# Hybrid HGRN2 and pooling block on one core: a third pair of banks for the transposes of the first tokens

## What is computed

```python
z = jnp.concatenate([meta, x], axis=1)
h = rms_norm(z, norm_w[l])
p = (h @ w_in[l] + b_in[l]).astype(f32)
q, fz, iv, g_hg, u, g_pool, m_hg, m_pool = jnp.split(p, split_at, axis=-1)
...
y_hg = (o * jax.nn.silu(g_hg)) @ w_down_hg[l].astype(f32)
...
merged = jax.nn.sigmoid(m_hg) * y_hg + jax.nn.sigmoid(m_pool) * y_pool
z = z + (merged @ w_out[l].astype(f32)).astype(z.dtype)
return rms_norm(z, final_norm_w)[:, N_META:]
```

## Time and profile before

| what | value |
|---|---|
| median of 3 runs | 1047.99 us (1047.74 to 1049.66) |
| the profiled execution's own time | 1047.79 us |
| its span, first to last instruction | 1046.1 us |
| granted clock of PE, mean | 0.999 |
| PE busy | 1025.0 us (98%) |
| DVE busy | 779.7 us (75%) |
| ACT busy | 491.4 us (47%) |
| POOL busy | 98.1 us (9%) |

### The profile page before, as it was taken

One profiled execution on the slowest core, in us unless ns is written; L12 is line 12 of the kernel. 1 busy time (PEld: TensorE's weight loads), 2 busy tenths in 40 slices (PEclk: granted clock), 3 DMA queues, 4 the chain that ended last, 5 costly groups with the idle time before them and its releaser, 6 DMA issues.

```text
span 1046.1 us, 18490 instructions
## 1 busy us (share of the span) xinstructions
PE 1025.0 (98%) x7252; PEld 835.8 (80%) x7252; DVE 779.7 (75%) x1276; ACT 491.4 (47%) x834; POOL 98.1 (9%) x166
## 2 busy tenths in 40 slices
PE   7999999999999999999999999999999999999997
PEld 7767888888888888878888887788887887787886
DVE  7989787878686868786676877764569789978234
ACT  7764636363636363544353433434457346345222
POOL 6200000000010101020101010011100110000111
PEclk9999999999999999999999999999999999999999
DMA  7221111111020202121312122228322684555233
GB/s 276 51 81 63 42 61 42 62 39 64 29 75 21 81 22 82 41 82 52 101 41 91 60 91 81 71 99 294 116 96 101 207 316 158 177 189 181 71 101 131
DMA packets 36630, 105.65 MB, mean 101 GB/s; under 512 B 4640, under 2 KB 4640, under 8 KB 36544
## 3 DMA queue, kind: packets, MB, share of 16 engines
q1 hardware_dynamic: 22352, 66.14, 19.5%
q0 software_dynamic: 8528, 27.31, 7.2%
q10 hardware_dynamic: 5664, 11.02, 2.9%
HBM read 79.28 MB, written 25.17 MB: 100 GB/s over the span
## 4 chain that ended last, share of the span: by engine, by line
PE 81%; DVE 13%; issue 3%; ACT 2%; DMA 1%; POOL 0%; DVEq 0%; SPq 0%; ACTq 0%
PE acc L1372 61%; PE acc L1259 8%; PE levels L1425 2%; DVE w_lo L1687 1%; PE miscs L1447 1%; PE miscs L1458 1%; PE miscs L1459 1%; DVE r_lo L2240 1%; PE acc L1317 1%; PE miscs L1259 1%; PE levels L1259 1%; DVE att L1841 1%; DVE qx L1860 1%; PE miscs L1465 1%; PE miscs L1438 1%
## 5 line engine op out<-in xcount | busy, mean ns | idle before, releaser
L1372 PE MATMUL acc<-r_hi,w_hi 128*128 128x512 f32 x1112 | 308.0, 399 | 4.1 <-ACT second L837 1.7
L1372 PE MATMUL acc<-r_lo,w_hi 128*128 128x512 f32 x1112 | 304.9, 393 | 0.5 <-DVE r_lo L2240 0.4
L1372 PE MATMUL acc<-r_hi,w_lo 128*128 128x512 f32 x1112 | 298.5, 390 | 0.5 <-DVE w_lo L1687 0.5
L1372 PEld LDWEIGHTS acc<-r_lo,w_hi 128*128 128x128 f32 x1112 | 206.5, 188 | 50.1 <-issue 4.9
L1372 PEld LDWEIGHTS acc<-r_hi,w_lo 128*128 128x128 f32 x1112 | 208.6, 188 | 45.6 <-DVE w_lo L1687 1.0
L1372 PEld LDWEIGHTS acc<-r_hi,w_hi 128*128 128x128 f32 x1112 | 201.6, 188 | 48.7 <-ACT second L837 3.1
L752 ACT ACTIVATE w_hi<-sum 128x512 fp32r<-128x512 f32 x156 | 97.8, 628 | 164.1 <-DVE sum L1721 85.7
L1687 DVE TENSOR_TENSOR w_lo<-sum,w_hi 128x512 fp32r<-128x512 f32 x156 | 106.3, 685 | 58.7 <-ACT w_hi L752 58.3
L1687 DVE TENSOR_TENSOR w_lo<-raws,w_hi 128x512 fp32r<-128x512 f32 x120 | 82.1, 686 | 54.8 <-ACT w_hi L752 54.6
L752 ACT ACTIVATE w_hi<-raws 128x512 fp32r<-128x512 f32 x120 | 74.5, 623 | 26.1 <-PE acc L1372 24.4
L837 ACT ACTIVATE second<-acc,bias 128x512 f32<-128x512 f32 x31 | 21.2, 684 | 57.8 <-PE acc L1372 57.7
(11 more groups left out here) (301 smaller groups left out, 1364.6 us busy)
## 6 DMA issues: line engine op xcount, KB each, us to landing
raws<-in_wstream SPq DMA_DIRECT2D x88, 512.0 KB, 3.6
xin<-in_x SPq DMA_DIRECT2D x8, 512.0 KB, 6.1
a_spill<-gt POOLq DMA_DIRECT2D x16, 256.0 KB, 3.5
c_spill<-pg POOLq DMA_DIRECT2D x16, 256.0 KB, 2.7
stage<-a_spill ACTq DMA_DIRECT2D x4, 1024.0 KB, 13.9
smh_spill<-zq POOLq DMA_DIRECT2D x16, 256.0 KB, 2.4
gate_in<-smh_spill SPq DMA_DIRECT2D x16, 256.0 KB, 5.2
part_spill<-zq POOLq DMA_DIRECT2D x16, 256.0 KB, 5.7
```

The lines of the kernel that those rows point to most:

```text
L1372: ins = pe.matmul(bank[:, :], weights, moving, start=n == 0 and i in (0, 1, 5 if p < EARLY else 3), stop=n == 3 * KH - 1, skip_group_check ...
```

## The change

Three engines get another order in the head; no arithmetic is added or taken away apart from two warm-up matmuls.
- Tile 3 is turned into `acc[3]` and `acc[2]`, two banks of the products. Tile 4 goes into the banks of tile 1 (`lev`, `small`), and from there on the even and odd tiles have changed places: 5 and 7 in `misc`, 6 and 8 in `lev` and `small`. `h_transposes(3)` no longer waits for another tile, and tile 4 waits, as tile 3 did, for tile 1. Product (0, 1) now also waits for `h_lo` of tile 3, since it overwrites `acc[2]`.
- DVE scales the rows of tile 3 before it splits tile 1, and the rows of tile 4 before it splits tile 2; the copies `b11_copy(3)` and `b11_copy(4)` come after other splits; `x_mean(5)` moves behind `low(1)`.
- ACT squares tile 5 after `high(1)` in place of before the copies of tile 3.
- PE issues four warm-up matmuls before product (0, 0) in place of six.

```diff
+        def tile_banks(i):
+
+            return (acc[3], acc[2]) if i == 3 else h_banks[i % 2 if i < 3 else (i + 1) % 2]
...
             first_tile(2)
-            square_x(5)
             first_tile(3)
             high(0)
             first_tile(4)
             high(1)
+            square_x(5)
             square_x(6)
...
                 elif p == 0 and i == 1:
                     pe.wait_ge(S["h_copied"], 4)
+                    pe.wait_ge(S["h_lo"], 3)
...
                     pe.wait_ge(S["hm_copied"], 1)
-                elif i > 2:
-                    pe.wait_ge(S["h_copied"], i - 2)
-                    pe.wait_ge(S["h_lo"], min(i - 2, 4))
+                elif i > 3:
+                    had = (1, 2, 4, 5, 6)[i - 4]
+                    pe.wait_ge(S["h_copied"], had)
+                    pe.wait_ge(S["h_lo"], min(had, 4))
...
-            keep_warm(6)
+            keep_warm(4)
             product(0, 0)
...
+            h_row(3)
             b11_low(1)
             b11_copy(1)
+            x_mean(4)
             b21_low(1)
-            h_row(3)
-            x_mean(4)
+            h_row(4)
             b11_low(2)
             b11_copy(2)
+            b11_low(3)
             b21_low(2)
-            h_row(4)
-            x_mean(5)
-            b11_low(3)
             low(0)
-            b11_copy(3)
             b11_low(4)
             b21_low(3)
+            b11_copy(3)
             b11_copy(4)
             b21_low(4)
             low(1)
+            x_mean(5)
             x_mean(6)
             h_row(5)
```

More of the change, by code:

```diff
@@ L761, in banks_of @@
             def banks_of(i, rows):
-                return [b[:, :].rearrange("p (k t) -> p k t", k=KH)[:, :, 0:rows] for b in h_banks[i % 2]]
+                return [b[:, :].rearrange("p (k t) -> p k t", k=KH)[:, :, 0:rows] for b in tile_banks(i)]
             def meta_tile():
@@ L1385, in h_transposes @@
                     pe.wait_ge(S["hm_copied"], 1)
-                elif i > 2:
-                    pe.wait_ge(S["h_copied"], i - 2)
-                    pe.wait_ge(S["h_lo"], min(i - 2, 4))
+                elif i > 3:
+                    had = (1, 2, 4, 5, 6)[i - 4]
+                    pe.wait_ge(S["h_copied"], had)
+                    pe.wait_ge(S["h_lo"], min(had, 4))
                 for k in range(NK):
                     o = (k % 4) * P
-                    ins = pe.transpose(h_banks[i % 2][k // 4][:, o:o + rows], hrow[0:rows, i % 2, k * P:(k + 1) * P],
+                    ins = pe.transpose(tile_banks(i)[k // 4][:, o:o + rows], hrow[0:rows, i % 2, k * P:(k + 1) * P],
                                        ident[0:rows, 0:rows])
@@ L1606, in banks_of @@
             def banks_of(i):
-                return [b[:, :].rearrange("p (k t) -> p k t", k=KH) for b in h_banks[i % 2]]
+                return [b[:, :].rearrange("p (k t) -> p k t", k=KH) for b in tile_banks(i)]
             def b11_low(i):
```

## The result

The changed kernel took 1050.19 us, median of 21 runs (1048.49 to 1051.37); the kernel before, run beside it, took 1048.78 us (1047.70 to 1049.66, 21 runs). The ratio is 1.0014, with a 95% interval from 1.0007 to 1.0020: slower by 1.4 us, inside 0.2%. The profiled execution took 1051.11 us, with a span of 1049.4 us: 3.3 us more than the span of before.

A forecast was written before the change was run, and what follows sets the result against it. The prediction took the head to be bounded by DVE before PE takes over; 0.63 us on PE's side and 0.65 to 0.8 on DVE's, side by side, gave +0.7 on 1047.99, so 1048.7 us, range 1046.9 to 1050.6.

The forecast's parts named there:

- The early start: Head: DVE scales tile 4 at 16.42 in place of 18.01, so product (0, 0) starts 1.97 us earlier, at about 19.55.
- What DVE still owes: Before tile 5: DVE's remaining work makes PE wait 0.8 us for `low(1)`, leaving about 1.0 of the 1.97 us.
- The mean that was moved: `x_mean(5)` on DVE: its power on POOL comes into the open, `h_row(5)` 0.89 us later, PE 0.63 us behind.
- POOL's queue: Three masks behind tile 5's late power hold up tile 6's: `h_row(6)` 1.4 us late, PE loses nothing more or 0.1.
- The wait for ACT at tile 8's split: DVE's old 0.62 us wait at 36.45 for ACT's last copy of tile 8, forecast to be filled by DVE's delay.
- The sum: Whole kernel: +0.7 us, from 0.63 on PE's side and 0.65 to 0.8 on DVE's, running side by side.
- The rival of the clock: PE's waits between 23.5 and 26.4 us make its clock fall: +2.55 us in all, 1050.5; chance 0.05.
- The prediction's own sign of the clock: Transposes after PE's stall before tile 5 longer than 1.1 us would show that the clock had fallen.
- hidden: Rival: POOL's power is done before DVE reaches `h_row(5)`, so nothing visible changes: -0.1 us, 1047.9; chance 0.08.
- slow: Rival: tile 5's power on POOL takes 1.52 us, 0.97 more on tile 5: +1.65 us, 1049.6; chance 0.07.
- the early start did not pass: Rival: PE's earlier start in the head passes through in full, -1.97 us, 1046.0; chance 0.05.
- the first mask held nothing: Rival: POOL's first mask holds `h_row(5)` until 25.27, 0.22 us more on tile 5: +0.9 us, 1048.9; chance 0.05.

The follow-up runs named there:

- E9: The changed kernel with thirteen warm-up matmuls in place of four ahead of product (0, 0): 1050.48 us, ratio 1.0016 to the kernel before.
- E1: The changed kernel with `x_mean(5)` moved up on DVE, ahead of `b21_low(4)`: 1048.98 us, ratio 1.0005 to the kernel before.
- E2: The changed kernel with POOL's three masks ahead of `x_rstd(5)` in place of behind it: 1049.95 us, ratio 1.0010 to the kernel before.
- E8: The changed kernel measured once more, with nothing altered: 1049.36 us, ratio 1.0009 to the kernel before.
- E5: The changed kernel with six throw-away warm-up matmuls ahead of tile 5's transposes: 1048.96 us, ratio 1.0008 to the kernel before.
- E10: The changed kernel with six throw-away matmuls ahead of tile 5's transposes, as E5, for more runs: 1049.53 us, ratio 1.0007 to the kernel before.
- E3: The changed kernel with twelve throw-away warm-up matmuls ahead of tile 5's transposes: 1051.55 us, ratio 1.0029 to the kernel before.
- E7: The changed kernel with `x_mean(5)`, `low(1)` and the masks earlier, `b11_copy(3)` and `b21_low(4)` later: 1047.67 us, ratio 0.9990 to the kernel before.

## Why the prediction was right, and where its size was off

**The verdict.** Within 0.2%, as forecast with 0.90. The measured step is +1.4 us, twice the forecast of +0.7, and the median of 1050.19 lies inside the range, near its end.

**The early start.** Right. Product (0, 0) at 19.64 (19.55 said), `h_row(4)` at 16.42 (16.42 said). Its worth was put at nothing, since PE's holes were DVE's work in another order; E9's head shows that.

**What DVE still owes.** Right. The two small means began at 24.21, where `x_mean(5)` was put at 24.23. PE waited 0.57 us for `low(1)` (0.8 said).

**The mean that was moved.** Right, and it is the whole of the regular loss. `h_row(5)` at 25.02 (25.05 said), tile 5 turned at 26.36 (26.39 said), the power 0.55 as taken from the idle row and not 1.52; PE stood 1.28 us (1.57 said). E1 undoes this step alone, and the head returns to that of before (+0.05).

**POOL's queue.** Right in the places: `h_row(6)` at 27.21 (27.3 said) behind a wait of 0.84, masks of 0.30 and 1.47 ahead of it. Its cost beside PE's delay is at most a tenth (E2). The wait for ACT at tile 8's split is gone in E8, as said; in the profile of the change it stands at 38.68 (0.88 us), where the slowed PE had made ACT's copy later still.
The Trainium skill (SBUF — State Buffer, "Who interferes with whom") would have had the first mask, begun at 24.95, hold `h_row(5)` for its whole length. The trace disagrees for that mask: the scaling began at 25.02 and took 1.28, and the second mask, begun at 25.20 under the scaling, was the one held; the third only queued behind it.

**The sum.** Right where the clock holds: +0.62 to +0.79 in the heads of E2, E5, E8, E9 and E10. As a forecast of the median it is short, at least in part because it took the fall of the clock as a rival for all runs or none, with 0.05, when it comes in a part of the executions: without the five runs of low clock the change has a median of 1049.59, 0.81 above before, and with them 1.41.

**The rival of the clock.** This is the step that was mis-sized. Its argument against itself, that holes of 1.77 and 1.06 us had left the transposes at 1.09, read those holes ahead of warm-ups; the new ones lie just behind the first products. Whether that difference is what decides, no run tests. The prediction's own sign of the clock, transposes of over 1.1 us behind the stall, came in the profile of the change (1.19 for tile 5, 1.39 for tile 6) and not in E8 (1.09 for tile 5). Runs with a mean clock of 0.997 or less number 11 of 43 in the three sets whose profile stands 1.28 us before tile 5 (the change, E8, E2), and none of 166 in all the others, before included. In the change these five have a median of 1050.59 and the sixteen others 1049.59; in E8, 1050.46 and 1049.08. So the counted runs are 1.0 to 1.4 us longer than the rest, which is no clean price, since the rest holds uncounted falls, that of the profiled run at least. In the head of the profiled one the fall cost 1.5 (2.20 - 0.7), against the 1.85 taken from the earlier trace rows, where the granted clock reads 1.00 and no row showed the lower level.
That the hole before tile 5 is what lets the clock fall is well supported, as E1, E3, E5, E9 and E10 each shorten or fill it and have no such run (none of 51); but only one trace shows where a fall lies. How much of the median's excess over +0.7 the clock makes is not settled: the very same kernel stood 1.41 us above before in its first comparison and 0.75 in E8, and the counts of falls alone (5 of 21 and 3 of 11) don't explain that difference. Falls too small for the count may: in the change the eleven runs at 0.999 have a median of 1049.29, 0.51 above before, and the five at 0.998 one of 1050.42; but in E8 the six at 0.998 have 1048.97 and the two at 0.999 have 1049.07. Why one execution falls and the next, with the same rows up to 26 us, does not, stays open.
The Trainium skill (TensorE: Matmul & The Clock Gate, "Part 1: The HAM clock gate") names idle gaps as what brings the lower level back, and as a plain rule it warns of gaps longer than any here. The trace of the change shows a fall, to 0.50, behind gaps of 0.57 and 1.28 us, and E8 shows the same gaps without one.

**The other rivals.** The power was neither hidden nor slow (0.55), the early start did not pass, the first mask held nothing.

## What to carry to other kernels

A small instruction that is moved counts by what it releases: the mean takes 0.15 us on DVE, but with its power on another engine and two hand-overs its reader needs some 0.7 us of other work in between (0.09 + 0.55 + 0.03). Where an engine's holes are another engine's work in a different order, starting it earlier only moves the hole; shorten what the other engine must do before the next reader, as E7 did. And a hole that moves, here from a stretch of warm-ups to behind the first products, can cost the clock in some executions, so read the granted clock of several runs and not of one profile.

## What was not expected of the hardware

The granted clock fell in some executions of one and the same program and not in others: 11 of 43 by the mean of the run, and the profiled one besides, where PE was busy 0.88 of 2.5 us shortly before it and had taken up its work again when the clock fell. In E9 a load of weights behind the head held ACT 2.95 us where it otherwise held it 0.7 to 1.0, in a kernel that differs only in throw-away matmuls some 46 us earlier. And PE's waits in the last stretch, for `zq`, `m` and `wo_lo`, differ by up to 1 us in all between profiles of kernels with equal heads, so of the 3.3 us by which the profiled spans differ a third says nothing on the change.
